# The GELU of a state-space mixer rewritten with tanh, and its gate tiles moved, in a one-core two-block kernel

## The reference, cut to what matters

```
y = gelu(y)                                    # 512 tokens x 512 features, tanh form of GELU
out = y * sigmoid(y @ w_glu + b_glu)           # the gate: a 512 x 512 matmul
h = h + concatenate([o_nsa, out], -1) @ w_out
```

## Time and profile before

| | before |
|---|---|
| median of 3 runs | 2016.18 us (2014.03 to 2018.53) |
| profiled execution | 2012.11 us, of which 2010.3 us are the span of the core's instructions |
| PE busy | 1938.9 us, 96% of the span |
| DVE busy | 1180.5 us, 59% |
| ACT busy | 846.1 us, 42% |
| granted TensorE clock, mean | 0.985 |

### The profile page before, as it was taken

One profiled execution on the slowest core, in us unless ns is written; L12 is line 12 of the kernel. 1 busy time (PEld: TensorE's weight loads), 2 busy tenths in 40 slices (PEclk: granted clock), 3 DMA queues, 4 the chain that ended last, 5 costly groups with the idle time before them and its releaser, 6 DMA issues.

```text
span 2010.3 us, 22343 instructions
## 1 busy us (share of the span) xinstructions
PE 1938.9 (96%) x8894; PEld 1508.5 (75%) x8894; DVE 1180.5 (59%) x1543; ACT 846.1 (42%) x1269; POOL 335.9 (17%) x329
## 2 busy tenths in 40 slices
PE   7999999999997999999999899999999899999997
PEld 5788888777643688888888777776788778766786
DVE  5758344576753456655655777925763559446732
ACT  5232233311576443313333438545542467455531
POOL 2000000144320011000111302603301024114002
PEclk9999999999999999999999899999999899999998
DMA  5332223222001145645542232221222222220231
GB/s 197 101 107 83 94 95 116 78 74 97 27 1 60 51 142 184 225 149 182 194 138 74 74 105 81 95 84 53 63 95 95 89 87 84 85 83 32 94 96 61
DMA packets 53463, 197.25 MB, mean 98 GB/s; under 512 B 6000, under 2 KB 6512, under 8 KB 52848
## 3 DMA queue, kind: packets, MB, share of 16 engines
q1 hardware_dynamic: 43200, 160.55, 24.1%
q0 software_dynamic: 7648, 29.10, 4.5%
q10 hardware_dynamic: 2512, 6.18, 0.9%
HBM read 192.67 MB, written 2.10 MB: 97 GB/s over the span
## 4 chain that ended last, share of the span: by engine, by line
PE 79%; DVE 11%; ACT 5%; issue 2%; POOL 2%; DMA 1%; ACTq 0%; POOLq 0%; DVEq 0%
PE PS L591 78%; DVE AR L1640 3%; DVE WLO L1637 2%; DVE AR L2148 1%; ACT WHI L1166 1%; PE PS L840 1%; DVE AR L1670 1%; DVE TMP L2222 1%; ACT HX L1331 0%; DVE AR L2115 0%; DMA H<-in_xT 0%; POOL ACC L2280 0%; DVE H L2051 0%; ACT SQ L1181 0%; POOL ACC L2399 0%
## 5 line engine op out<-in xcount | busy, mean ns | idle before, releaser
L591 PE MATMUL PS<-HNH,WHI 128*128 128x512 f32 x1632 | 656.7, 402 | 16.4 <-ACT HNH L1197 14.6
L1637 DVE TENSOR_TENSOR WLO<-RAW,WHI 128x1024 fp32r<-128x1024 f32 (+1 forms) x272 | 374.7, 1380 | 505.8 <-ACT WHI L1166 505.7
L591 PE MATMUL PS<-HNH,WLO 128*128 128x512 f32 x1632 | 639.1, 392 | 5.6 <-DVE WLO L1637 5.6
L1166 ACT ACTIVATE WHI<-RAW 128x1024 fp32r<-128x1024 f32 (+1 forms) x272 | 297.6, 1095 | 643.7 <-PE PS L591 581.3
L591 PE MATMUL PS<-HNL,WHI 128*128 128x512 f32 x1632 | 436.2, 390 | 0.1
L591 PEld LDWEIGHTS PS<-HNH,WHI 128*128 128x128 f32 x1632 | 307.8, 189 | 95.9 <-issue 21.8
L591 PEld LDWEIGHTS PS<-HNH,WLO 128*128 128x128 f32 x1632 | 308.1, 189 | 80.2 <-issue 9.1
L591 PEld LDWEIGHTS PS<-HNL,WHI 128*128 128x128 f32 x1632 | 307.3, 188 | 64.9 <-DVE HNL L1640 1.0
L2280 POOL TENSOR_TENSOR ACC<-ACC,SQ 128x512 f32<-128x512 f32 x46 | 62.2, 1352 | 814.4 <-ACT SQ L1181 813.4
L591 PE MATMUL PS<-AR 32*128 32x256 f32 (+14 forms) x844 | 167.4, 412 | 1.2 <-DVE AR L1640 0.6
L591 PE MATMUL PS<-HIDH,WLO 128*128 128x512 f32 x352 | 137.0, 389 | 0.0
(11 more groups left out here) (311 smaller groups left out, 2314.7 us busy)
## 6 DMA issues: line engine op xcount, KB each, us to landing
RAW<-in_w_in SPq DMA_DIRECT2D x80, 512.0 KB, 3.5
AR<-in_w_ada POOLq DMA_DIRECT2D x48, 512.0 KB, 4.0
RAW<-in_w13a SPq DMA_DIRECT2D x44, 512.0 KB, 3.3
RAW<-in_w13b SPq DMA_DIRECT2D x44, 512.0 KB, 4.1
RAW<-in_w_out SPq DMA_DIRECT2D x40, 512.0 KB, 3.4
RAW<-in_w2a SPq DMA_DIRECT2D x16, 704.0 KB, 4.0
RAW<-in_w2b SPq DMA_DIRECT2D x16, 704.0 KB, 4.7
RAW<-in_w_inA SPq DMA_DIRECT2D x12, 512.0 KB, 3.3
```

The source lines that it names most:

```text
L591: return pe.matmul(o, l, r, start=start, stop=stop, skip_group_check=True)
L1166: act.activation(hi_of(name, i), raw_of(name, i), ACT.Copy).then_inc(*HI.up(name, i))
L1637: dve.tensor_tensor(lo_of(name, i), raw_of(name, i), f32(hi_of(name, i)), S_).then_inc(*LO.up(name, i))
```

## The change

The GELU is spelled out. For tile m, DVE computes U*U, then times 0.044715 plus 1, then times U, in `S5T[m]` (step `cube`); ACT takes the tanh; DVE multiplies (1 + tanh) with U (step `gelu`). The factor 0.5 of the GELU is carried into the later constants. `cube` m is in round 15+m, `gelu` m in round 16+m, ahead of that round's `cube`. The gate tiles are in rounds 20, 22, 24 and 26, and `s5_out` in rounds 28 and 29. The number of instructions on PE stays, and the order of the weight loads too.

```diff
-        if n == 23:
+        if n == 15:
             assert next(s5, None) is None
-            yield ("gelu",)
-        if 24 < n < 29:
-            yield "glu", n - 25
-        if n in (29, 30):
-            yield "s5_out", 2 * n - 58
-            yield "s5_out", 2 * n - 57
+        if 15 < n < 20:
+            yield "gelu", n - 16
+        if 14 < n < 19:
+            yield "cube", n - 15
+        if n in (20, 22, 24, 26):
+            yield "glu", (n - 20) // 2
+        if n in (28, 29):
+            yield "s5_out", 2 * n - 56
+            yield "s5_out", 2 * n - 55
...
# PE, step "glu"
-                    pe.wait_ge(*A.at("gelu", 3))
+                    pe.wait_ge(*V.at("gelu", 3))
...
# ACT
                 elif step == "gelu":
-                    for m in range(4):
-                        act.wait_ge(*V.at("read", 2 * m + 1))
-                        act.activation(U[:, m, :], U[:, m, :], ACT.Gelu_apprx_tanh).then_inc(*A.up("gelu", m))
+                    m, = at_
+                    act.wait_ge(*V.at("cube", m))
+                    act.activation(S5T[m], S5T[m], ACT.Tanh, scale=float(np.sqrt(2 / np.pi))).then_inc(*A.up("gelu_tanh", m))
...
# ACT, step "glu": scale=0.5 of the tanh becomes 0.25; step "s5_out": scale=0.5 becomes 0.25
# DVE
+                elif step == "cube":
+                    m, = at_
+                    dve.wait_ge(*P_.at("read", 7))
+                    dve.wait_ge(*V.at("read", 2 * m + 1))
+                    dve.tensor_tensor(S5T[m], U[:, m, :], U[:, m, :], M_).then_inc(*V.up("cube"))
+                    mine()
+                    dve.tensor_scalar(S5T[m], S5T[m], 0.044715, 1.0, M_, A_).then_inc(*V.up("cube"))
+                    mine()
+                    dve.tensor_tensor(S5T[m], S5T[m], U[:, m, :], M_).then_inc(*V.up("cube", m))
+                elif step == "gelu":
+                    m, = at_
+                    dve.wait_ge(*A.at("gelu_tanh", m))
+                    stt(U[:, m, :], S5T[m], 1.0, U[:, m, :], A_, M_).then_inc(*V.up("gelu", m))
...
# DVE, step "low": 0.5 becomes 0.25
```

More of the change, by code:

```diff
@@ L1373, in act_program @@
                     act.wait_ge(*V.at("half_b"))
-                    act.activation(S5T[m], bank("w_glu", m)[:, :], ACT.Tanh, bias=HALF_B[:, m:m + 1], scale=0.5).then_inc(*A.up("glu", m))
+                    act.activation(S5T[m], bank("w_glu", m)[:, :], ACT.Tanh, bias=HALF_B[:, m:m + 1], scale=0.25).then_inc(*A.up("glu", m))
                 elif step == "s5_out":
@@ L1377, in act_program @@
                     act.wait_ge(*V.at("s5_out", m))
-                    act.activation(pairs_of(OH[:, 4 + m, :]), in_order(U[:, m, :]), ACT.Copy, scale=0.5).then_inc(*A.up("part", 4 + m))
+                    act.activation(pairs_of(OH[:, 4 + m, :]), in_order(U[:, m, :]), ACT.Copy, scale=0.25).then_inc(*A.up("part", 4 + m))
                 elif step == "o_part":
@@ L2020, in dve_program @@
                         mine()
-                        stt(pairs_of(OL[:, k, :]), in_order(U[:, k - 4, :]), 0.5, pairs_of(f32(OH[:, k, :])), M_, S_).then_inc(*V.up("part", k))
+                        stt(pairs_of(OL[:, k, :]), in_order(U[:, k - 4, :]), 0.25, pairs_of(f32(OH[:, k, :])), M_, S_).then_inc(*V.up("part", k))
                 elif step == "values" and at_[0] == 3 and at_[1:] == [2, 2]:
```

## The result

The kernel after took 2029.54 us as the median of 7 runs (2022.98 to 2031.98), the kernel before 2016.18 us (2013.94 to 2018.53, 7 runs): 13.4 us more, a ratio of 1.0063 with a 95% interval of 1.0051 to 1.0074. The forecast was 2023.2, its range 2013.0 to 2028.5. The sign was right, the size too small, and the time lies 1.0 us above the range. The profiled execution took 2031.65 us with a span of 2029.9.

What follows compares the result with a forecast made beforehand. PE was taken to bound on average (79% of the waits), but the changed rounds as a ring across PE, DVE and ACT. +8.3 -3.4 +4.1 -1.4 = +7.6, less 0.6, on 2016.18 gave 2023.2 us; range 2013 to 2028.5.

Steps and rivals of the forecast that it cites:

- A, the ring: Rounds 15 to 19: spelled-out GELU in DVE's queue lengthens the loop of PE, DVE and ACT, +8.3 us.
- the walk: Hop-by-hop estimate of PE's times from gate tile 0 (608.5) to values of unit 27 (661.7): +9.0 us.
- B, table and lump: Round 23: ACT loses the GELU and its two table loads, 4.75 us in one lump; -3.4 us.
- C, the gates: Gate tiles every second round: ACT's load waits leave PE without cover behind tiles 1 to 3; +4.1 us.
- the clock rival: PE's new gaps of 2 us or more each cost 1.3 us of slow clock; +12 us, 2028; chance 0.17.
- D: s5_out a round earlier: one pair leaves round 30, where PE waited for ACT's scaling; -1.4 us.

Runs made afterwards that it cites:

- GELU part alone: Kernel after with gate tiles back in rounds 25 to 28 and s5_out in 29 and 30, spelled-out GELU kept; 2019.35 us, ratio 1.0010.
- late splits: Kernel after with the splits of w_out's first tiles called a round later than their gate tiles; 2015.03 us, ratio 0.9988 against before.
- The filler: Kernel after with three unused fp32 products of constants on PE in each of its three idle stretches; 2024.78 us, ratio 1.0044 against before.
- gate part alone: Kernel before with table GELU moved to round 19, gate tiles in rounds 20, 22, 24, 26, s5_out in 28 and 29; 2025.06 us, ratio 1.0038.

## Why the prediction was right in kind and wrong in size

- **A, the ring.** Predicted: share of unit 19 8.3 us late, the shares 5.3 us apart. Measured: 610.80 - 600.49 - 3.47 = 6.8 late, and 5.0 to 5.7 apart in three of the four rounds (the fourth, without a cube, 4.0). The mechanism was right, the price a little too dear: a cube took up 1.79 us of the queue and a multiplication 0.61, priced at 1.9 and 0.7, and the four rounds took 20.0 us where 21.3 had been added up. The claim that place in the queue decides more than busy time held: with the same DVE instructions and the tanh waited for a round later, the four rounds took 15.2 us in place of 20.0. There was luck in it too. Gate tile 0 began 1.1 us earlier than in the walk (607.4 for 608.5) and then took 5.12 us for the 3.95 allowed, so that it ended at 612.5 as forecast: two errors cancelled, and the second was the clock.
- **B, table and lump.** Predicted -3.4. In the GELU part alone the stretch was +3.8 with a share 6.8 late, so B and what follows gave -3.0 by subtraction, close to the forecast. The kernel after has no table load from 535 to 725 us, as foreseen.
- **C, the gates.** The mechanism was right to the gap: predicted idle 4, 3 and 3 us behind tiles 1 to 3, measured 4.20, 3.68 and 3.57; ACT's waits, foreseen at 3 to 6 us, were 5.07, 7.16 and 5.20. The size was off, and this is **the step that failed**: the 0.3 us of slow clock allowed for a gate tile (tile 2 in the walk: 4.0 us) and the durations at full clock for what stands behind the gaps. Tile 2 took 5.63 us, the values behind the next gap 3.25 and not 1.65. By the walk's marks, less 3.47: tile 1's end 621.0 (walk 621.6), transposes of unit 22 627.8 (628.4), tile 2's end 635.8 (634.1), values of unit 23 642.1 (640.4), tile 3's end 651.4 (647.4), transposes of unit 26 658.7 (654.6), values of unit 27 668.79 - 3.47 = 665.3 (661.7), transposes of unit 30 674.3 (670.5). All of the 3.8 us missing come between tile 2's start and tile 3's, where PE ran at a granted clock of 0.65 over the tile and of 0.50 from the values (645.59) to tile 3 (651.16): tile 2 took 1.6 us more than in the walk, the values 1.6, transposes and scores 0.7.
- **Why it was mis-sized.** I had the clock as a rival, priced at +5, and set against it that slow matmuls hide where ACT or DVE is late. That argument was half right: in part A slow matmuls hide, since in the kernel after, the GELU part and late splits the transposes of unit 15 took 1.27, 1.73 and 1.57 us and the four rounds 20.0 each time. But the slow spells behind tiles 1 and 2 begin where PE resumes, and what PE does there includes a gate tile, which ACT's next load waits for. They lay on the path. The filler showed this: 5.6 us back for more work. The stretch's +11.5 lies in the clock rival's band, +9.5 to +15, which had been given a chance of 0.17.
- The Trainium skill, "TensorE: Matmul & The Clock Gate", Terms, prices the gate as the throttled time times the share of pulses withheld. As an estimate by that rule, the mean clock of 0.80 over 92.3 us against 0.89 over 80.9 makes 18.5 against 8.9 us, 9.6 more. PE's busy time grew by 7.7, so the rule comes out higher than the trace; it counts low clock in idle time too. It needs the clock of the trace after, and could not have given the forecast.
- **D** could not be told by itself. The last wait was 1.71 us in place of 2.88, near the 1.5 foreseen.
- **The last 1.9 us.** 13.4 at the medians against 11.5 in the stretch. With the stretch alone the time would have been 2016.2 + 11.5 = 2027.7, inside the range. The kernel after in a second series was at 2026.12, +9.0, so the 1.9 us are within what series differ by; no run gives them a cause. The 0.6 us taken off the sum for overlap in A was there (the four rounds came out 1.3 us shorter than added up), and the clock outweighed it.

Two things stay open. The first is why the slow spells behind gaps of the same length were shorter with the gate part alone. The second is why three of the kernel after's eight later runs took 2018 to 2019 us while the other five took 2024.7 to 2032.6. Over the whole execution the granted clock was 0.980 to 0.983 in the three and 0.977 to 0.980 in the five, so the clock goes with it; but no profile of a short run was taken.

## What to carry to other kernels

On an engine that works in order, price an added operation by what stands behind it in the queue until the next thing another engine waits for; 10 us of work in 11 us of idle time cost 6.8 us here, and with only the multiplication one round further on four rounds took 1.2 us more than before in place of 6.0. Where a step waits for a load that a step just ahead of it has set off, put a round between them. And where a change makes PE idle for a few microseconds, look in the trace for what the same work takes at the lower clock, and count it on the path if another engine's wait hangs on that work; here it was 2.0 us on a gate tile and 1.6 us on the values.

## What the runs showed that I had not expected

- Useless matmuls in PE's gaps made the stretch 5.6 us shorter, where 2.3 to 3.8 had been expected, with the mean clock at 0.88 and not 0.80.
- A 0.16 us instruction of DVE lasted up to 1.22 us while GpSimd was in a tensor_tensor, and ended with it.
- GpSimd's cube took 3.2 us a tile, so that four were done in four rounds. Its rows (timeline of the version with all of the GELU's multiplications on GpSimd):

```profile
585.17 1.04 POOL L2326 TENSOR_TENSOR SQ<-AR 128x512 f32<-128x512 f32 x1 [2.36 <-PE PS L594]
586.31 0.62 POOL L2328 TENSOR_SCALAR SQ<-SQ 128x512 f32<-128x512 f32 x1
587.01 1.28 POOL L2330 TENSOR_TENSOR SQ<-SQ,AR 128x512 f32<-128x512 f32 x1
```

- The same code outside the stretch took 1929.5 to 1938.0 us from profile to profile, 8.5 us apart, which is more than most of the differences in time in the table.
